# Sharing the scaled one-hots with GpSimd, reading PSUM in the gate stages, and fewer rank compares in the expert lookups

## The reference, cut to what matters

```
s = einsum('thsk,hsnk->thsn', qr, sub_keys)        # two score rows of 128 keys
top_s, top_i = lax.top_k(s, 16)                    # 16 best keys of each row, by rank
cand_s = top_s[:, :, 0, :, None] + top_s[:, :, 1, None, :]
best_s, best_j = lax.top_k(cand_s, 16)             # 16 best pairs: "picks"
idx  = cand_i at best_j      # = top_i[first][rank a] * 128 + top_i[second][rank b]
gate = softmax(best_s)
out  = sum over picks of gate * gelu(token . expert_u[idx]) * expert_v[idx]
```

## Time and profile before

| | |
|---|---|
| median of three runs | 3216.91 us |
| profiled execution: time / span | 3221.7 us / 3219.9 us |
| mean granted TensorE clock | 0.948 of full speed |
| busy: TensorE, VectorE, ScalarE, GpSimd | 90%, 70%, 41%, 6% of the span |
| gate stage of layer 0, first compare to first expert work on ScalarE | 789.0 to 922.4 us |
| gate stage of layer 1, the same | 2490.1 to 2556.6 us |

### The profile page before, as it was taken

One profiled execution on the slowest core, in us unless ns is written; L12 is line 12 of the kernel. 1 busy time (PEld: TensorE's weight loads), 2 busy tenths in 40 slices (PEclk: granted clock), 3 DMA queues, 4 the chain that ended last, 5 costly groups with the idle time before them and its releaser, 6 DMA issues.

```text
span 3219.9 us, 49255 instructions
## 1 busy us (share of the span) xinstructions
PE 2907.5 (90%) x17089; PEld 2405.6 (75%) x17089; DVE 2261.6 (70%) x4424; ACT 1332.8 (41%) x2254; POOL 200.1 (6%) x238
## 2 busy tenths in 40 slices
PE   7999999864789999999999998977891899999998
PEld 5655544553679999999999997766780788888887
DVE  3264442869987777777777776366439988888887
ACT  3122221122974444444444443131311966666664
POOL 0000000000001111111111110000000000001010
PEclk8999999775999999999999999998995999999999
DMA  5522112724247878878777775133241188888886
GB/s 229 193 85 80 64 66 78 274 95 177 98 171 250 290 263 284 288 255 293 249 253 257 248 252 188 63 112 102 90 144 41 48 321 315 315 317 314 315 313 222
DMA packets 164476, 645.09 MB, mean 200 GB/s; under 512 B 15616, under 2 KB 49568, under 8 KB 125216
## 3 DMA queue, kind: packets, MB, share of 16 engines
q1 hardware_dynamic: 135520, 434.15, 38.8%
q0 software_dynamic: 28864, 209.76, 17.7%
HBM read 624.02 MB, written 19.79 MB: 200 GB/s over the span
## 4 chain that ended last, share of the span: by engine, by line
PE 79%; DVE 12%; ACT 7%; DMA 1%; issue 1%; POOL 0%; SPq 0%; ACTq 0%; DVEq 0%
PE ps L694 78%; ACT hot L1450 3%; DVE topi L1861 1%; DVE topi L1869 1%; DVE sc L1863 1%; ACT spill L1442 1%; ACT gateA L1439 1%; DVE top L1858 1%; DVE top L1866 1%; ACT gateB L1436 1%; PE ps L802 0%; DVE besti L1869 0%; DVE eq L1905 0%; DVE eq L1901 0%; DVE cand L1863 0%
## 5 line engine op out<-in xcount | busy, mean ns | idle before, releaser
L694 PE MATMUL ps<-h2a,ehi 128*128 128x384 f32 x2048 | 521.7, 335 | 1.4 <-DVE elo L1956 1.4
L1490 ACT ACTIVATE ehi<-ring 128x1024 fp32r<-128x1024 f32 x256 | 271.5, 1060 | 359.9 <-PE ps L694 359.5
L1991 DVE TENSOR_TENSOR elo<-ring,ehi 128x1024 fp32r<-128x1024 f32 x256 | 313.1, 1223 | 104.5 <-ACT ehi L1490 104.5
L694 PEld LDWEIGHTS ps<-h2a,ehi 128*128 128x128 f32 x2048 | 373.0, 188 | 11.7 <-DVE elo L1956 1.9
L694 PE MATMUL ps<-h2b,ehi 128*128 128x192 f32 x2048 | 349.6, 274 | 1.8 <-DVE elo L1956 1.8
L694 PE MATMUL ps<-h2a,elo 128*128 128x384 f32 x1024 | 343.7, 336 | 0.0
L694 PEld LDWEIGHTS ps<-h2b,ehi 128*128 128x128 f32 x2048 | 322.5, 193 | 13.2 <-DVE elo L1956 2.1
L1956 DVE TENSOR_TENSOR elo<-ring,ehi 128x1024 fp32r<-128x1024 f32 x256 | 311.9, 1219 | 12.4 <-ACT ehi L1463 12.4
L694 PE MATMUL ps<-hT,ring 128*128 128x512 f32 (+1 forms) x896 | 308.3, 503 | 0.0
L677 POOL DMA_INDIRECT gbuf<-in_expert_rows,gidx x192 | 183.4, 955 | 1788.6 <-DVE yg L1979 1651.4
L694 PE MATMUL ps<-h2b,elo 128*128 128x192 f32 x1024 | 282.4, 276 | 0.0
(11 more groups left out here) (326 smaller groups left out, 4518.0 us busy)
## 6 DMA issues: line engine op xcount, KB each, us to landing
ring<-in_experts SPq DMA_DIRECT2D x512, 512.0 KB, 5.2
ring<-in_w_mod SPq DMA_DIRECT2D x48, 1024.0 KB, 7.6
ring<-in_w_side SPq DMA_DIRECT2D x24, 1024.0 KB, 5.0
ring<-in_w_front SPq DMA_DIRECT2D x12, 1024.0 KB, 7.3
ring<-in_w_merge SPq DMA_DIRECT2D x16, 768.0 KB, 4.3
ring<-in_w_q SPq DMA_DIRECT2D x12, 1024.0 KB, 4.8
gate_scratch<-spill SPq DMA_DIRECT2D x48, 256.0 KB, 2.0
gateA<-gate_scratch SPq DMA_DIRECT2D x4, 3072.0 KB, 21.4
```

The lines of the kernel that those rows point to most:

```text
L694: return pe.matmul(out, w, x, start=start, stop=stop, **k)
L1490: act.activation(ehi[:, 2 + k % 2, :], ring[:, (u + k) % RING, DM:2 * DM], ACT.Copy).then_inc(vhi_ready, 1)
L1991: v.tensor_tensor(elo[:, r, DM:2 * DM], ring[:, r, DM:2 * DM], ehi[:, 2 + b, :].bitcast(F32), ALU.subtract).then_inc(vlo_ready, 1)
```

## The change

In the route stages the 256 columns are laid out by pick first (`k t h` in place of `t k h`), so that picks 0 to 7 of both token blocks are the first 128 columns. Those are compared with ranks 0 to 7 only; picks 8 to 15 with all 16. The multiplication becomes three instructions and the first halving add covers the late columns alone.

In the gate stages GpSimd makes the scaled one-hot of token 3 of each group, VectorE that of token 2, and ScalarE scales tokens 0 and 1. VectorE reads `iota` from PSUM bank 0, where ScalarE puts it at the beginning of the stage. GpSimd issues its first two gathers in the gate stage, ahead of the one-hots, and the rest in the expert stage as before. TensorE waits for GpSimd's one-hot (`hot_pool`) too.

```diff
 @block.gpsimd, kind == "gates" (was: part of "experts")
                     pool.wait_ge(pick_col, routes_by(l))
+                    for k in range(2):
+                        gather(l, k)
+                    pool.wait_ge(x_held, 16 * (l + 1))
+                    for n in range(dense_tokens(l) // 4):
+                        k = 4 * n + 3
+                        count(pool, gate_ps, gb + n - 3)
+                        pool.tensor_scalar(hot[:, n % 4, 1, 3, :], iota, idxT[:, 1, k:k + 1], idxT[:, 2, k:k + 1],
+                                           ALU.is_equal, ALU.mult).then_inc(hot_pool, 1)
...
 @block.tensor, gates
                             pe.wait_ge(hot_times, i * 4 + (gb + g + 1))
+                            pe.wait_ge(hot_pool, i * 4 + (gb + g + 1))
...
 @block.scalar, gates
+                    act.wait_ge(pick_col, routes_by(l))
+                    act.activation(ps[:, 0, 0:P], iota, ACT.Copy).then_inc(iota_ready, 1)
                     for n in range(ng):
                         act.wait_ge(hot_eq, gb + n + 1)
-                        for t in range(3):
+                        for t in range(2):
...
 @block.vector, route
-                    link(v.tensor_copy(place[:, :].rearrange("p (t k h) -> p t k h", t=2, k=TOPK),
+                    link(v.tensor_copy(place[:, :].rearrange("p (k t h) -> p t k h", t=2, k=TOPK),
...
-                    link(v.tensor_tensor(eq[:, :, :, :], rank[:, :, :].unsqueeze(2).to_broadcast([P, 2, TOPK, w]),
-                                         nth[:, :, :].unsqueeze(1).to_broadcast([P, 2, TOPK, w]), ALU.is_equal))
+                    for k, c in ((TOPK // 2, slice(0, hw)), (TOPK, slice(hw, 2 * hw))):
+                        last = v.tensor_tensor(eq[:, :, 0:k, c], rank[:, :, c].unsqueeze(2).to_broadcast([P, 2, k, hw]),
+                                               nth[:, 0:k, c].unsqueeze(1).to_broadcast([P, 2, k, hw]), ALU.is_equal)
+                    link(last)
...
+                    v.tensor_tensor(late_, late_, tops.to_broadcast([P, 2 * TOPK, TOPK // 2, 2 * NH]), ALU.mult)
+                    for s_ in range(2):
+                        early = eq[:, s_, 0:TOPK // 2, 0:hw].rearrange("p k (j m) -> p k j m", j=TOPK // 2)
+                        part = tops[:, TOPK * s_:TOPK * s_ + TOPK // 2]
+                        last = v.tensor_tensor(early, early, part.to_broadcast([P, TOPK // 2, TOPK // 2, 2 * NH]), ALU.mult)
+                    link(last)
+                    link(v.tensor_tensor(eq[:, :, 0:8, hw:2 * hw], eq[:, :, 0:8, hw:2 * hw], eq[:, :, 8:16, hw:2 * hw], ALU.add))
-                    for n in (8, 4, 2):
+                    for n in (4, 2):
...
 @block.vector, gates
+                    dve.wait_ge(iota_ready, l + 1)
+                    row = ps[:, 0, 0:P]
                     for n in range(dense_tokens(l) // 4):
-                        g, k = n % 4, 4 * n + 3
+                        g, k = n % 4, 4 * n + 2
...
-                        v.tensor_tensor(hot[:, g, 1, 0:3, :], iota.unsqueeze(1).to_broadcast([P, 3, P]),
+                        v.tensor_tensor(hot[:, g, 1, 0:2, :], row.unsqueeze(1).to_broadcast([P, 2, P]),
...
-                        v.tensor_scalar(hot[:, g, 1, 3, :], iota, idxT[:, 1, k:k + 1], idxT[:, 2, k:k + 1],
+                        v.tensor_scalar(hot[:, g, 1, 2, :], row, idxT[:, 1, k:k + 1], idxT[:, 2, k:k + 1],
                                         ALU.is_equal, ALU.mult)
-                        v.tensor_tensor(hot[:, g, 0, :, :], iota.unsqueeze(1).to_broadcast([P, 4, P]),
+                        v.tensor_tensor(hot[:, g, 0, :, :], row.unsqueeze(1).to_broadcast([P, 4, P]),
```

More of the change, by code:

```diff
@@ L429, in build_program @@
             sem("exp_in"), sem("exp_out"), sem("pick_ready"), sem("pick_ps"), sem("pick_col"))
-        hot_eq, hot_times = sem("hot_eq"), sem("hot_times")
+        hot_eq, hot_times, hot_pool, iota_ready = sem("hot_eq"), sem("hot_times"), sem("hot_pool"), sem("iota_ready")
         hot_ready, gate_ps, gate_ready = sem("hot_ready"), sem("gate_ps"), sem("gate_ready")
@@ L650, in _, with gather @@
         def _(pool):
+            def gather(l, k):
+                at = NK - gathers(l) + k
+                pool.indirect_dma_start(gbuf[:, k % 2, :], None, a[f"expert_rows{l}"],
+                                        bass.IndirectOffsetOnAxis(gidx[:, at:at + 1], 0)).then_inc(gather_in[k % 2], 16)
             for st in stages:
@@ L664, in _ @@
                         pool.dma_start(a["x_scratch"], xT[:, :, :]).then_inc(x_held, 16)
-                elif kind == "experts":
-                    gn, first = gathers_before(l), NK - gathers(l)
+                elif kind == "gates":
+                    gb, first = groups_before(st), NK - gathers(l)
+                    idxT = peer_tiles(l)[1]
                     pool.wait_ge(gidx_ready, l + 1)
@@ L673, in _ @@
                     pool.wait_ge(pick_col, routes_by(l))
[L674 to L679, removed]
+                    for k in range(2):
[6 more added lines that the diff above has]
+                                           ALU.is_equal, ALU.mult).then_inc(hot_pool, 1)
+                elif kind == "experts":
+                    for k in range(2, gathers(l)):
+                        pool.wait_ge(acc_done, gathers_before(l) + k - 1)
+                        gather(l, k)
                     lo_, up_ = slice(0, KD // 2), slice(KD // 2, KD)
@@ L1897, in _ @@
                     link(v.tensor_tensor(rb, rb, place[:, :], ALU.add))
-                    w = 2 * NH * TOPK
+                    hw = NH * TOPK
                     dve.wait_ge(nth_ready, l + 1)
-                    link(v.tensor_tensor(eq[:, :, :, :], rank[:, :, :].unsqueeze(2).to_broadcast([P, 2, TOPK, w]),
-                                         nth[:, :, :].unsqueeze(1).to_broadcast([P, 2, TOPK, w]), ALU.is_equal))
-                    e4 = eq[:, :, :, :].rearrange("p s k (t j h) -> p (s k t) j h", t=2, j=TOPK)
@@ L1904, in _ @@
-                    t4 = topf[:, :, :, :, :].rearrange("p s k t h -> p (s k t) h").unsqueeze(2)
-                    link(v.tensor_tensor(e4, e4, t4.to_broadcast([P, 4 * TOPK, TOPK, NH]), ALU.mult))
-                    for n in (8, 4, 2):
+                    for k, c in ((TOPK // 2, slice(0, hw)), (TOPK, slice(hw, 2 * hw))):
+                        last = v.tensor_tensor(eq[:, :, 0:k, c], rank[:, :, c].unsqueeze(2).to_broadcast([P, 2, k, hw]),
+                                               nth[:, 0:k, c].unsqueeze(1).to_broadcast([P, 2, k, hw]), ALU.is_equal)
@@ new lines, in _ @@
+                    link(last)
+                    tops = topf[:, :, :, :, :].rearrange("p s k t h -> p (s k) (t h)").unsqueeze(2)
+                    late_ = eq[:, :, :, hw:2 * hw].rearrange("p s k (j m) -> p (s k) j m", j=TOPK // 2)
+                    v.tensor_tensor(late_, late_, tops.to_broadcast([P, 2 * TOPK, TOPK // 2, 2 * NH]), ALU.mult)
[3 more added lines that the diff above has]
+                        last = v.tensor_tensor(early, early, part.to_broadcast([P, TOPK // 2, TOPK // 2, 2 * NH]), ALU.mult)
@@ L1907, in _ @@
+                    link(last)
+                    link(v.tensor_tensor(eq[:, :, 0:8, hw:2 * hw], eq[:, :, 0:8, hw:2 * hw], eq[:, :, 8:16, hw:2 * hw], ALU.add))
+                    for n in (4, 2):
                         link(v.tensor_tensor(eq[:, :, 0:n, :], eq[:, :, 0:n, :], eq[:, :, n:2 * n, :], ALU.add))
                     for s_ in range(2):
-                        last = v.tensor_tensor(pick[:, :, s_, :], eq[:, s_, 0, :].rearrange("p (t m) -> p t m", t=2),
-                                               eq[:, s_, 1, :].rearrange("p (t m) -> p t m", t=2), ALU.add)
+                        last = v.tensor_tensor(pick[:, :, s_, :].rearrange("p t (j h) -> p t j h", h=NH),
+                                               eq[:, s_, 0, :].rearrange("p (j t h) -> p t j h", t=2, h=NH),
+                                               eq[:, s_, 1, :].rearrange("p (j t h) -> p t j h", t=2, h=NH), ALU.add)
```

2 lines of the change are left out of this document (1 added, 1 removed).

## The result

The changed kernel took 3194.82 us (median of 4 runs, 3190.71 to 3196.78), the kernel before 3217.72 us in the same comparison (4 runs): 22.9 us less, ratio 0.9927, interval 0.9914 to 0.9939. Timed once more with the experiments it was 3195.68 against 3215.40 us, ratio 0.9936 (0.9922 to 0.9949). The forecast was 16.8 us less, 3200 us, and faster by more than 0.2%: right in direction and inside its range, 6.1 us short in size.

The account below looks back on a forecast made before the run. TensorE is busy 90% of the span, but VectorE and ScalarE were taken to fill the gate stages, and VectorE's lookups to lie on the routes' path. Lookups 9.0 plus gates 7.8 gave 16.8 us less, 3200 us, range 3187 to 3213.

Parts of the forecast that it names:

- The lookups, 9.0 us: Route stages: shorter compare, multiply and first halving add on VectorE save 3.0 us a route, 9.0 us in three.
- A group, 1.26 us: Gate stages: VectorE needs 1.26 us a group, compares paying nothing for PSUM, the tensor_scalar 0.067 us more.
- GpSimd hidden, 0.6 us: Gate stages: GpSimd's one-hot takes 0.6 us, hidden behind VectorE's 1.26, and decides only once over 1.26.
- The beginning, 1.7 and 2.5 us: Start of the gate stages: TensorE waits for GpSimd behind its gathers; VectorE stands 1.7 us in layer 0, 2.5 in layer 1.
- The sign to look for: Start of both gate stages: TensorE should start at the second gather's end and VectorE stand for 2 to 3 us.
- The end, 2.8 us: End of each gate stage: ScalarE's expert work begins 2.8 us after VectorE's last group, in both layers.
- Sum of the gate stages, 7.8 us: Both gate stages together 7.8 us less: 7.5 in layer 0, 0.3 in layer 1.
- The expert stage begins earlier with the same work.: After the gate stages nothing new is late: the expert stage begins earlier, its work unchanged.
- GpSimd near or over VectorE's rate: Two gate-stage rivals: GpSimd at 1.30 to 1.42 us a group, 3206 to 3223 us, chance 0.09; at 1.5, 3235, chance 0.06.
- PSUM reads dearer in this pattern: Gate-stage rival: each PSUM read of a broadcast row costs VectorE 0.065 us on three instructions, 28 us, 3228; chance 0.03.
- lookups losing the fast rate: Route-stage rival: shorter pieces leave the fast rate and the lookups gain nothing, 9 us less gain, 3209; chance 0.04.
- The rival of the same sign: Gate-stage rival: tensor_scalar keeps its rate, 8.6 us less, or VectorE never stands, 4.2 less, or both: 3187 to 3196; chance 0.17.

Follow-up runs that it names:

- e5: Kernel before, all three VectorE instructions of a gate group reading iota from PSUM, nothing given to GpSimd: 3225.05 against 3219.32 us, ratio 1.0019.
- e6: Changed kernel, VectorE's tensor_scalar alone reading iota from SBUF, the compares from PSUM: 3183.66 us against 3219.32 for the kernel before, ratio 0.9896.
- e1: Kernel before with the route edits only: 3209.06 us against 3217.89, ratio 0.9973.
- e7: Changed kernel, GpSimd making the scaled one-hots of tokens 2 and 3, VectorE only compares: 3244.53 us, ratio 1.0077 to the kernel before.
- e4: Changed kernel, GpSimd's first two gathers moved behind its first four one-hots in both layers: 3197.14 us, ratio 0.9940 to the kernel before.
- e3: Changed kernel, VectorE reading iota from SBUF again in all three instructions, GpSimd's share kept: 3198.61 us, ratio 0.9937 to the kernel before.

## Why the prediction was right, and where it was short

- **What bounds the stages.** Right. VectorE ran without a gap before and after; a tensor_scalar 0.064 us longer (e5) or 0.055 us shorter (e6) moved the group's distance by 0.054 and 0.063 us.
- **The lookups, 9.0 us.** Right: 3.0 us in each of the three routes, e1 8.8 us. Each piece came out as worked out from the fixed 0.16 us and 0.52 ns an element.
- **A group, 1.26 us.** Right: 1.25. Compares pay nothing for PSUM, the tensor_scalar 55 to 64 ns (0.067 forecast).
- **GpSimd hidden, 0.6 us.** Right in effect; 0.79 us in fact. No row had priced it, and the nearest one, a memset, was a poor guide: VectorE's 1.25 us forgave an error of a third. That it decides once it needs more than VectorE was confirmed by e7.
- **The beginning, 1.7 and 2.5 us.** Mis-sized: 1.3 and 0.84 us. The gather rows shrank from 1.51 and 1.43 to 1.04 and 0.96 us (e5 has it too, with nothing given to GpSimd; the PSUM operand and VectorE's later start both have a part, see there), so GpSimd's first one-hot came 2.8 us after the first compare and not 3.7, and TensorE began after 3.8 us, not 4.3. I took over a duration from a row whose surroundings the change alters. In layer 1 the wait was a third of the forecast, since the two later waits didn't come: TensorE's first four groups took 5.24 us there, about as long as the 5.43 of layer 0 before, because the granted clock was 0.75 from 2477.8 to 2479.8 and 1.00 after, where before it had stayed at 0.50 to 0.62 for the first six us. What raised it sooner was not taken apart. The sign to look for, 2 to 3 us of stand in both stages, came in neither, and didn't fit the forecast's own 1.7 us.
- **The end, 2.8 us.** 2.3 us in both layers: with ScalarE ahead it is shorter than it was in layer 1 before.
- **Sum of the gate stages, 7.8 us.** 10.0 + 3.5 less 0.45 and 0.48 us for `iota` (0.4 forecast) is 12.5. Of the 4.7 us missed, 1.7 are 0.012 us in 144 groups, 2.1 the beginning and 1.0 the end; `iota` took 0.1 back.
- **"The expert stage begins earlier with the same work."** The same work, but not the same clock: 2.6 us less in layer 1, which no step of the forecast had. It is luck: e4 and e6 are small edits of the changed kernel, and e4 has none of it and e6 1.5 us.
- **Rivals.** GpSimd near or over VectorE's rate, PSUM reads dearer in this pattern, lookups losing the fast rate: none came. The rival of the same sign (VectorE never standing, tensor_scalar at its rate) named the two places where more was to be had. The measured 3194.8 us lies between the 3187 and 3196 given to it, but the tensor_scalar did lose its rate, and the beginning was covered only in part: 2.1 of its 4.2 us came. The rest came from the groups, the end and the clock, all to the same side.

## What to carry to other kernels

Where one engine has no gap for a hundred groups, price an edit by the distance between its starts, and check the other engines' distances for the point at which they take over. Choose where each operand lies instruction by instruction: here `iota` for the two-operand compares belongs in PSUM, because they then don't hold GpSimd up and lose nothing, and for the tensor_scalar in SBUF, because from PSUM it loses its fast rate; one rule for all three cost 8 us of the stages with everything in PSUM and 11 us with everything in SBUF. Before a duration is taken over from the trace, ask whether the change also alters what made it long.

## What the runs showed of the hardware

- A tensor_scalar of 128 fp32 elements takes 0.79 us on GpSimd, 0.777 us from start to start back to back (e7). Beside VectorE compares with two SBUF operands it takes 1.26 us (e3), and 0.93 us when it starts together with a tensor_scalar of VectorE's at the fast rate (e6).
- Issuing an indirect gather took 0.96 to 1.08 us in the record in every kernel whose compares read PSUM, the ones with the tensor_scalar from SBUF included. With the compares from SBUF it took 1.43 to 1.54 us in the kernel before and e1; in e3 it took 1.94 us once and 0.98 to 1.04 three times, so the slowing depends on more than the operand, when VectorE starts for one.
- TensorE's granted clock in the first 4 us of full work after layer 1's gate stage was 0.50 before and 1.00 after the change, though the 4 us directly in front were equally idle; the expert stage of 640 us was 2.6 us shorter with it. A busier gate stage alone doesn't bring it (e4: 54.0 of 62.2 us busy, 0.50).
